# The low parts of the weights move from 64 to 192 bytes past the start of their slots, in the blocks of the two-width form

## The reference

```python
def reference(...):
    for l in range(DEPTH):                                   # DEPTH = 2
        h = rms_norm(x, pre_mix_norm[l])
        h = hybrid_mixer(h, positions, w_in[l], ..., w_out[l])   # attention and SSD side by side
        x = x + rms_norm(h, post_mix_norm[l])
        h = rms_norm(x, pre_mlp_norm[l])
        h = jnp.square(jax.nn.relu(h @ w_up[l])) @ w_down[l]
        x = x + rms_norm(h, post_mlp_norm[l])
    return x
```

## Time and profile before

| what | value |
|---|---|
| median of 3 runs | 2192.64 us (2191.41 to 2193.32) |
| the profiled execution | 2192.87 us, of which the span of its instructions is 2191.1 us |
| TensorE matmuls | 2175.8 us busy, 99% of the span, 11449 matmuls |
| TensorE weight loads | 1869.8 us, 85%, beside the matmuls |
| VectorE | 1368.3 us, 62% |
| ScalarE | 1022.6 us, 47% |
| GpSimd | 105.2 us, 5% |
| mean granted clock of TensorE | 0.998 of full speed |

### The profile page before, as it was taken

One profiled execution on the slowest core, in us unless ns is written; L12 is line 12 of the kernel. 1 busy time (PEld: TensorE's weight loads), 2 busy tenths in 40 slices (PEclk: granted clock), 3 DMA queues, 4 the chain that ended last, 5 costly groups with the idle time before them and its releaser, 6 DMA issues.

```text
span 2191.1 us, 32251 instructions
## 1 busy us (share of the span) xinstructions
PE 2175.8 (99%) x11449; PEld 1869.8 (85%) x11449; DVE 1368.3 (62%) x1633; ACT 1022.6 (47%) x1314; POOL 105.2 (5%) x105
## 2 busy tenths in 40 slices
PE   9999999999999999999999999999999999999998
PEld 8888888888888888888898888888888888888886
DVE  6988464764555465556588875657555645554655
ACT  6544464643444344344455445546434434443443
POOL 2051000000000000000001410000000000000000
PEclk9999999999999999999999999999999999999999
DMA  6655556656666656665556555556666566656664
GB/s 210 182 154 172 154 191 193 192 181 203 186 195 193 193 179 200 193 187 189 183 157 184 157 169 153 196 179 194 201 193 192 175 208 179 203 193 191 174 208 146
DMA packets 232841, 404.31 MB, mean 185 GB/s; under 512 B 12508, under 2 KB 62452, under 8 KB 232244
## 3 DMA queue, kind: packets, MB, share of 16 engines
q1 hardware_dynamic: 231780, 398.57, 59.3%
q10 hardware_dynamic: 720, 4.26, 0.5%
q0 software_dynamic: 256, 0.33, 0.1%
HBM read 401.01 MB, written 2.10 MB: 184 GB/s over the span
## 4 chain that ended last, share of the span: by engine, by line
PE 98%; issue 0%; DMA 0%; DVE 0%; ACT 0%; SPq 0%; POOL 0%; POOLq 0%; DVEq 0%; ACTq 0%
PE wide L975 21%; PE wide L856 16%; PE wide L858 16%; PE wide L857 16%; PE wide L983 11%; PE wide L926 8%; PE wide L933 4%; PE wide L1112 1%; PE wide L907 1%; PE wide L909 1%; PE wide L910 1%; PE wide L1014 1%; PE wide L1133 0%; DMA raw<-in_w_in 0%; PE wide L1153 0%
## 5 line engine op out<-in xcount | busy, mean ns | idle before, releaser
L1331 DVE TENSOR_TENSOR w_lo<-raw,w_hi 128x1024 fp32r<-128x1024 f32 x752 | 926.5, 1242 | 705.5 <-ACT w_hi L556 660.8
L556 ACT ACTIVATE w_hi<-raw 128x1024 fp32r<-128x1024 f32 x752 | 788.3, 1058 | 898.4 <-PE wide L858 478.8
L856 PE MATMUL wide<-w_hi,u_hi 128*128 128x512 f32 x1280 | 498.5, 389 | 0.0
L858 PE MATMUL wide<-w_hi,u_lo 128*128 128x512 f32 x1280 | 498.0, 389 | 0.0
L857 PE MATMUL wide<-w_lo,u_hi 128*128 128x512 f32 x1280 | 497.9, 389 | 0.0
L975 PE MATMUL wide<-a_both,w_hi 128*128 128x512 f32 x2032 | 486.3, 391 | 0.0
L975 PEld LDWEIGHTS wide<-a_both,w_hi 128*128 128x128 f32 x2032 | 373.2, 188 | 72.1
L858 PEld LDWEIGHTS wide<-w_hi,u_lo 128*128 128x128 f32 x1280 | 240.2, 188 | 49.9
L857 PEld LDWEIGHTS wide<-w_lo,u_hi 128*128 128x128 f32 x1280 | 240.3, 188 | 49.8
L856 PEld LDWEIGHTS wide<-w_hi,u_hi 128*128 128x128 f32 x1280 | 240.2, 188 | 49.6
L983 PEld LDWEIGHTS wide<-a_both,w_lo 128*128 128x128 f32 x2032 | 257.3, 189 | 9.6
(11 more groups left out here) (248 smaller groups left out, 1366.4 us busy)
## 6 DMA issues: line engine op xcount, KB each, us to landing
raw<-in_w_up SPq DMA_DIRECT2D x256, 512.0 KB, 3.9
raw<-in_w_down SPq DMA_DIRECT2D x256, 512.0 KB, 4.5
raw<-in_w_in SPq DMA_DIRECT2D x176, 512.0 KB, 3.7
raw<-in_w_out SPq DMA_DIRECT2D x64, 512.0 KB, 4.4
zg<-in_post_mix_norm ACTq DMA_DIRECT2D x2, 1024.0 KB, 5.0
zg<-in_post_mlp_norm ACTq DMA_DIRECT2D x2, 1024.0 KB, 6.9
out<-x_sb SPq DMA_DIRECT2D x8, 256.0 KB, 2.5
x_sb<-in_x SPq DMA_DIRECT2D x3, 512.0 KB, 8.8
```

The costliest lines, as they stand in the source:

```text
L556: act.activation(w_hi[:, c % RING], raw[:, c % RING], ACT.Copy).then_inc(sem["hi_ready"], 1)
L856: pe.matmul(o, sh, wh, start=(k == 0), stop=False)
L858: ins = pe.matmul(o, sl, wh, start=False, stop=(k == KT - 1))
L1331: dve.tensor_tensor(lo[:, c % RING], raw[:, c % RING], hi[:, c % RING].bitcast(F32), ALU.subtract).then_inc(sem["split_done"], 1)
```

## The change

One constant. `SHIFT` counts numbers of 4 bytes: 16 of them are 64 bytes, 48 are 192 bytes.

```diff
-SHIFT, ROOM = 16, 128
+SHIFT, ROOM = 48, 128
```

## The result

The kernel after took 2197.62 us (2196.34 to 2199.36, 10 runs), the kernel before 2192.65 us in as many (2191.12 to 2194.28): a ratio of 1.0023, 95% interval 1.0015 to 1.0032. It is slower by 5.0 us. The profiled execution has a span of 2196.2 us against 2191.1. The instructions and their order are the same.

A forecast was written before the change was run, and what follows sets the result against it. The prediction took TensorE's matmul pace as the bound. VectorE's writes, the wait and the low-weight loads were each put at 0, summing to no change: 2192.6 us, range 2179.5 to 2199.

The forecast's parts named there:

- The bound: Two-width blocks: TensorE never waits for operands, so only the pace of its matmuls can move the time.
- VectorE's part: VectorE's split writes landing 128 bytes further on: 0 on the path, at most 3.5 us if its idle cover were gone.
- the wait of L1330: Wait of the first three chunks: same count, still covers the shifted slot's reach into the next; 0.
- 276, 281 and 283 ns: Durations of one low-matmul shape in a fast half-block run, up blocks and the first block; read as no fixed price.
- two reads meet there: In SBUF, reads of the stream and of the next weights meet now and then, depending on places and timing.
- The down blocks and the first block: Control sign: down blocks must stay at 21.76 us, the first block's L910 at 283 ns.
- the one on the high matmuls: 16 high matmuls in 3.65 us, 0.02 us per pair over streaming rate: kept at 0, bound 3.5 us either side.
- the dearer form of rival 2: Low matmuls at 120 ns with the high ones disturbed for longer too, 3.5 us more: 2201 us, outside the range.
- The dt weights: Dt-weight loads at steps of 128 bytes, alike at 276 ns; taken to show 192 bytes no worse than 64 by itself.
- Rival 3: Places repeat every 128 bytes, so 64 and 192 are the same: 2192.6 us; chance 0.44 together with the forecast.
- Rival 2: Every low run: loads at 192 bytes meet the stream in each matmul, 120 ns each, +5.3 us, 2198 us; chance 0.22.
- Rival 1: Every low run settles at the streaming rate, 1.81 us for 16, 276 ns: 2180.5 us; chance 0.34 with partial forms.

The follow-up runs named there:

- e5: Against the kernel before: VectorE writes the low parts at 192 bytes, TensorE still loads them at 64 (part of the low product wrong); 2193.86 us.
- e6: Kernel before with 128 empty bytes ahead of `w_hi`, which move `w_hi`, `w_lo` and `a_both` together, SHIFT still 16; 2193.03 us.
- e9: Kernel before with `a_both` 64 bytes further on and SHIFT 32: low weights still 64 bytes from the stream, high ones 192 instead of 0; 2208.07 us.
- e8: Kernel after (SHIFT 48) with each chunk doing its 8 high matmuls and then its 8 low ones, so twice as many handovers; 2199.18 us.
- e15: Kernel after (SHIFT 48) with `a_both` 128 bytes further on: low distance 64 again, high distance 128 instead of 0; 2202.48 us.
- e1: Kernel before with the low parts not shifted at all (SHIFT 0); 2196.04 us.
- e2: Kernel before with SHIFT 32, a low shift of 128 bytes; 2196.45 us.
- e3: Kernel before with SHIFT 80, a low shift of 320 bytes (64 + 256); 2191.29 us.
- e10: Kernel before with `a_both` 192 bytes further on and SHIFT 64: low and high weights both 64 bytes from the stream; 2195.21 us.
- e16: Kernel before with SHIFT 56, a low shift of 224 bytes; 2191.24 us in a single run.
- e4: Kernel before with SHIFT 144 and ROOM 256, a low shift of 576 bytes (64 + 512); 2193.07 us.

## Why the prediction was wrong

The forecast was 2192.6 us and no change; measured were 2197.62 us and 0.23% slower. The range of 2179.5 to 2199 holds it. The direction and the likeliest case were wrong, and the loss is just above the 4.4 us that the prediction called distinguishable.

**What held.** The bound: TensorE's pace, with no idle time in the two-width blocks. VectorE's part and the wait of L1330 at nothing, which e5 shows directly for the writes. That 276, 281 and 283 ns depend on the places of both loads and stream in memory (e6, e9) and on what came ahead (e8, e15). That two reads meet there is an explanation which no run shows directly. The down blocks and the first block stayed.

**The step that failed** is the one on the high matmuls: "They load `w_hi`, whose place stays, so I keep them at 0 and let the bounds stand." The bound beside it, 3.5 us to either side, was also too small: their groups grew by 4.2 us (L975) and 0.6 (L926). In the up blocks they carry all of the loss, 3.653 to 3.688 us in a run of 16, +0.035 us, while the low runs gained 0.003; in the half blocks the low matmuls add 0.4 us, which includes the end of the two fast runs. I had the mechanism in hand for one direction only. The prediction says that the low runs' pace comes from the phase in which they are entered. The same trace had the other direction, since the five slow high matmuls stand directly behind the low run; its rows showed the sum, 3.65 us and not 3.627. Taking that 0.02 us as a constant of the high weights was the error. Only the dearer form of rival 2 let the high ones be disturbed for longer, on top of a price for the low ones, and the range left that form out.

**The dt weights.** That four places alike at 276 ns make 192 "not a worse place than 64 by itself" held for the low runs, 1.884 us against 1.887. It said nothing of a low run that hands over to 16 matmuls of 512 columns, where the loss arose. As evidence for no change it was too weak for the weight that I gave it. Rival 3, a period of 128 bytes, is refuted by e1 against e2 and by the change itself; the period is 256 bytes (e3).

**The rivals.** Rival 2's 2198 us is 0.4 us off, by a price that wasn't paid: its condition, 120 ns in each low matmul, was not met (118 ns, 1.884 us), and its signs, 1.92 us, 283 ns and weight loads of 192 ns in all of L983, did not show. That it names the right sum is chance. The 120 ns are what an unshifted low run costs (e1). Rival 1's state exists (e10: 276 ns, 1.82 us), but e10's high run lost more, 3.729 us for 3.653, than its low run won.

**What stays open** is the law by which a distance and an entry give the next state. The runs show what it depends on (distance modulo 256 bytes of both sorts of weights, and what the run ahead hands on); none of the values of e9 to e16 could be computed beforehand. What in the chip holds the matmuls up is open as well. A place at which high and low runs both go at the streaming rate (5.44 us for two chunks against 5.54; the best found has 5.53) is not among the eleven pairs of distances that were run.

## What to carry to other kernels

Where TensorE is busy for all of the time and each matmul loads new weights, the distance in memory between the loaded and the streamed operand was worth up to 0.7% of the time here (e9, 2208.07 against 2193.04 us). Treat it as something to sweep over one period, not to derive, and judge each value by the lengths of stages in the trace, which repeat within 0.05 us where whole times differ by 2. When a change touches one operand, price its neighbours in the instruction stream too: a run of matmuls hands its state to the next, and the cost can show in instructions whose own operands didn't move.

## What the runs showed of the hardware

- At a granted clock of 1.00 fp32r streams at 226.7 ns for 512 columns (96 matmuls in 21.76 us) and 113.3 for 256 (16 in 1.813 us) where nothing holds it up. Other matmuls of these blocks, each with its own weight load beside it, last up to 11 ns longer at 256 columns (276 ns of duration, 287 in e2) and 14 ns at 512 (389 before, 403 after), and some loads take 192 ns in place of 188.
- The pace depends on the distance between load and stream modulo 256 bytes, not on the place itself (e3, e4 and e6, 88.64 us for four up blocks as before), and not on where VectorE writes (e5, 88.64). The Trainium skill has it differently: "TensorE: Matmul & The Clock Gate", section "Step-by-step: what each phase is for", says that the loading of the next weights takes no read bandwidth from the running matmul. In these runs the pace of the running matmuls does depend on where the loaded weights lie: 233.5 ns for each of 16 matmuls in a row in e9, 3.736 us against 3.627 at the streaming rate. Whether read bandwidth is what they lack isn't shown.
- The pace depends on what came ahead: one layout shows two lengths in turn (e8: 1.82 and 1.86 us in the high run; e15: 1.89 and 1.82 us in the low run).
